# The first gate tile of each layer moved ahead of the transposes of the latents

## What is computed

```python
def token_mix(h, pos, w_in, lb, hg_norm_g, q_norm_g, w_q_up, kv_norm_g, w_kv_up, w_br_a, w_br_b, w_out):
    proj = h @ w_in
    hq, hf, hi, hgate, cq, ckv, kr, gates = jnp.split(proj, IN_SPLITS, axis=-1)
    o_a = hgrn2_mix(hq, hf, hi, lb)             # a recurrence, in levels
    ...
    y_b = mla_mix(cq, ckv, kr, pos, q_norm_g, w_q_up, kv_norm_g, w_kv_up) @ w_br_b
    g = jax.nn.sigmoid(gates.astype(jnp.float32))
    g_a, g_b = g[..., :D], g[..., D:]
    merged = (g_a * y_a + g_b * y_b)
    return merged @ w_out

def mla_mix(c_q, c_kv, k_rope, pos, q_norm_g, w_q_up, kv_norm_g, w_kv_up):
    q = (rmsnorm(c_q, q_norm_g) @ w_q_up)       # 384 latent columns
    kv = (rmsnorm(c_kv, kv_norm_g) @ w_kv_up)   # 256 latent columns
    ...
```

## Time and profile before

| | |
|---|---|
| median of 3 runs | 1886.56 us (1885.85 to 1888.33) |
| the profiled execution | 1887.39 us |
| its span | 1885.7 us |
| TensorE matmuls busy | 1693.9 us, 90% of the span |
| VectorE busy | 1184.9 us, 63% |
| ScalarE busy | 975.0 us, 52% |
| GpSimd busy | 26.7 us, 1% |
| moved by DMA | 401.83 MB, 213 GB/s over the span |

### The profile page before, as it was taken

One profiled execution on the slowest core, in us unless ns is written; L12 is line 12 of the kernel. 1 busy time (PEld: TensorE's weight loads), 2 busy tenths in 40 slices (PEclk: granted clock), 3 DMA queues, 4 the chain that ended last, 5 costly groups with the idle time before them and its releaser, 6 DMA issues.

```text
span 1885.7 us, 26698 instructions
## 1 busy us (share of the span) xinstructions
PE 1693.9 (90%) x10028; PEld 1408.3 (75%) x10028; DVE 1184.9 (63%) x1669; ACT 975.0 (52%) x1365; POOL 26.7 (1%) x58
## 2 busy tenths in 40 slices
PE   6999897899996989886899999979898769999995
PEld 6999785499995968743688888869695357888884
DVE  5544355554447444723788888854574378888886
ACT  4444344154434423401788888744341049888883
POOL 2000000000000000001000000000000010000000
PEclk9999998999998989998799999989899969999998
DMA  8555478845552559722398998935332308898992
GB/s 255 191 188 178 154 244 279 272 156 190 178 190 88 169 169 348 267 89 89 113 335 314 333 329 319 331 110 166 125 112 89 112 32 297 316 332 325 324 335 76
DMA packets 245831, 401.83 MB, mean 213 GB/s; under 512 B 6522, under 2 KB 151596, under 8 KB 245756
## 3 DMA queue, kind: packets, MB, share of 16 engines
q1 hardware_dynamic: 244792, 398.77, 61.6%
q0 software_dynamic: 592, 0.93, 0.2%
q10 hardware_dynamic: 372, 1.07, 0.2%
HBM read 399.70 MB, written 1.05 MB: 213 GB/s over the span
## 4 chain that ended last, share of the span: by engine, by line
PE 82%; DVE 10%; ACT 4%; issue 2%; DMA 1%; ACTq 0%; DVEq 0%
PE bank L1226 19%; PE bank L1168 14%; PE bank L1250 9%; PE bank L1097 8%; PE bank L1075 8%; PE bank L1181 6%; PE bank L1063 4%; PE bank L1262 3%; PE bank L1333 2%; DMA sb_ring<-in_w_in 1%; PE bank L1508 1%; PE bank L1086 1%; PE bank L1579 1%; DVE sb_w_lo L1808 1%; DVE sb_w_lo L1873 1%
## 5 line engine op out<-in xcount | busy, mean ns | idle before, releaser
L1873 DVE TENSOR_TENSOR sb_w_lo<-sb_ring,sb_moe_hi 128x1024 fp32r<-128x1024 f32 x384 | 448.4, 1220 | 29.5 <-ACT sb_moe_hi L697 29.2
L697 ACT ACTIVATE sb_moe_hi<-sb_ring 128x1024 fp32r<-128x1024 f32 x384 | 381.5, 1056 | 69.8 <-PE bank L1250 33.7
L1829 DVE TENSOR_TENSOR sb_w_lo<-sb_ring,sb_w_hi 128x1024 fp32r<-128x1024 f32 x128 | 151.1, 1222 | 172.1 <-ACT sb_w_hi L652 172.1
L1168 PE MATMUL bank<-sb_hT_hi,sb_w_hi 128*128 128x256 f32 x704 | 200.6, 285 | 3.6 <-DVE sb_hT_lo L1785 3.6
L652 ACT ACTIVATE sb_w_hi<-sb_ring 128x1024 fp32r<-128x1024 f32 x128 | 128.4, 1051 | 144.6 <-PE bank L1168 131.1
L1168 PE MATMUL bank<-sb_hT_hi,sb_w_lo 128*128 128x256 f32 x704 | 200.4, 285 | 0.0
L1168 PE MATMUL bank<-sb_hT_lo,sb_w_hi 128*128 128x256 f32 x704 | 200.4, 285 | 0.0
L1226 PE MATMUL bank<-sb_moe_hi,sb_xw_hi 128*128 128x512 f32 x480 | 193.6, 403 | 0.0
L1226 PE MATMUL bank<-sb_w_lo,sb_xw_hi 128*128 128x512 f32 x480 | 190.9, 398 | 0.0
L1226 PE MATMUL bank<-sb_moe_hi,sb_xw_lo 128*128 128x512 f32 x480 | 190.2, 396 | 0.0
L1250 PE MATMUL bank<-sb_moe_hi,sb_hid_hi 128*128 128x512 f32 x512 | 145.4, 396 | 2.9 <-DVE sb_hid_hi L1899 2.9
(11 more groups left out here) (465 smaller groups left out, 3132.9 us busy)
## 6 DMA issues: line engine op xcount, KB each, us to landing
sb_ring<-in_w_up SPq DMA_DIRECT2D x64, 1024.0 KB, 5.3
sb_ring<-in_w_gate SPq DMA_DIRECT2D x64, 1024.0 KB, 5.3
sb_ring<-in_w_down SPq DMA_DIRECT2D x64, 1024.0 KB, 4.8
sb_ring<-in_ada_w SPq DMA_DIRECT2D x48, 1024.0 KB, 7.7
sb_ring<-in_w_in SPq DMA_DIRECT2D x46, 1024.0 KB, 5.3
sb_ring<-in_ffn_w_in SPq DMA_DIRECT2D x44, 1024.0 KB, 5.0
sb_ring<-in_ffn_w_out SPq DMA_DIRECT2D x22, 1024.0 KB, 4.9
sb_ring<-in_w_out SPq DMA_DIRECT2D x12, 1024.0 KB, 5.0
```

Of the source, the lines that this page charges most:

```text
L697: A(moe_hi[:, q % 3, c], ring[:, at % RING, c], ACT.Copy).then_inc(s["moe_hi"], 1)
L1168: ins = mm(bank[4 + 2 * p + b][:, jj * SEQ:(jj + 1) * SEQ], w[wp][:, k, jj * P:(jj + 1) * P], h_parts[hp][:, k, :], start=k == 0 and m == ...
L1829: ins = tt(w_lo[:, slot, c], ring[:, slot, c], w_hi[:, q % 2, c].bitcast(F32), ALU.subtract)
L1873: ins = tt(w_lo[:, slot, c], ring[:, slot, c], moe_hi[:, q % 3, c].bitcast(F32), ALU.subtract)
```

## The change

The product with `gates0` is issued right behind `misc2`, before the wait for `latents`, into bank 3 instead of bank 0. Its eviction stands behind the square root and before the wait for the transposes. TensorE waits for that eviction before `kv_up` writes banks 0 to 3. In the list of tiles `gates0` comes right behind `misc2`. Step 0 keeps its `ada` products, its level and its part of the attention.

```diff
@@ -333,11 +333,14 @@
             for n in range(3):
                 tile(f"misc{n}.{l}", cols(w2, 2048 + MISC_AT[n], FB))
+            gates = lambda n: tile(f"gates{n}.{l}", cols(w2, 2048 + MISC + n * FB, FB))
+            gates(0)
             for n in range(2):
                 tile(f"q_up{n}.{l}", cols(a["w_q_up_2"][l], n * QL, QL))
             tile(f"kv_up.{l}", cols(a["w_kv_up_2"][l], 0, 1024))
             for n in range(8):
-                tile(f"gates{n}.{l}", cols(w2, 2048 + MISC + n * FB, FB))
+                if n:
+                    gates(n)
@@ -927,7 +930,13 @@
+                def gate_out(n, src):
+                    used(f"gates{n}.{l}")
+                    A(G[:, :, n // 4, (n % 4) * FB:(n % 4 + 1) * FB],
+                      src[:, :].rearrange("p (t c) -> p t c", t=T), ACT.Tanh, scale=0.5).then_inc(s["gates"], 1)
+
                 root(next(roots))
+                gate_out(0, bank[3])
                 act.wait_ge(s["cT"], run)
@@ -944,10 +953,8 @@
                 for n, L in enumerate(LEVELS):
 
-                    used(f"gates{n}.{l}")
-                    ins = A(G[:, :, n // 4, (n % 4) * FB:(n % 4 + 1) * FB],
-                            bank[n % 3][:, :].rearrange("p (t c) -> p t c", t=T), ACT.Tanh, scale=0.5)
-                    ins.then_inc(s["gates"], 1)
+                    if n:
+                        gate_out(n, bank[n % 3])
@@ -1490,6 +1497,7 @@
                 by_token(f"misc2.{l}", bank[2], hT_lo_l)
 
+                by_token(f"gates0.{l}", bank[3], hT_lo_l)
                 pe.wait_ge(s["latents"], run)
@@ -1508,6 +1516,7 @@
                     ins.then_inc(tiles_used, 1)
+                pe.wait_ge(s["gates"], 8 * l + 1)
                 pos = place[f"kv_up.{l}"]
@@ -1562,7 +1571,8 @@
-                    by_token(f"gates{n}.{l}", bank[n % 3], hT_lo_l)
+                    if n:
+                        by_token(f"gates{n}.{l}", bank[n % 3], hT_lo_l)
```

## The result

The change made the kernel faster, by less than was predicted: 1875.56 us median (12 runs, 1871.79 to 1883.5) against 1888.18 us for the kernel before (12 runs, 1885.49 to 1893.8), a ratio of 0.9937 with a 95% interval of 0.9925 to 0.995. That is 11.9 us (9.4 to 14.2); 18.6 had been predicted. The profiled execution took 1880.98 us, its span 1879.3. Timed again, beside the first experiments, the ratio was 0.9927 (0.9905 to 0.995), 13.8 us.

A forecast was written before the change was run, and what follows sets the result against it. The prediction took the chain of waits, 82% of it TensorE, to bound the kernel. Gains of 9.5 us in layer 0 and 9.1 in layer 1 make 18.6 us, so 1868.0 us, range 1865.0 to 1876.0.

The forecast's parts named there:

- The moved product: gates0's product, 5.94 (5.86) us, fits TensorE's 6.4 us gap before the latents transposes, with about 0.5 us left.
- The moved eviction: The Tanh on ScalarE, between the root and the latents' copies, costs 0, with a margin of 1.0 us.
- The clock: Full clock through the latents transposes and q_up: gains of 3.55 us in layer 0 and 4.05 in layer 1.
- The first rival: Chance 0.20: TensorE gets 1.2 GHz in the transposes or part of q_up, losing 1 to 7.6 us; 1869.5 to 1875.5.
- After kv_up: Behind kv_up gates0's 5.94 (5.86) us leave, the 2.41 us wait stays; layer 1 waits 0.7 us before gates1.
- Layer 0's loads: Layer 0's gate tile loads land 9.5 to 10.2 us earlier, so layer 0 keeps its 9.5 us gain.
- the prediction's own signs of being wrong: Transposes waiting beyond the latents' scaling, q_up showing 0.50, or layer 0's gates ending less than 8 us earlier.
- The sum: Over both layers, 9.5 + 9.1 = 18.6 us gained, giving 1868.0 us.
- The other rivals: Layer 0's loads eat its gain (0.10, 1877.5), larger gain (0.05, 1864), slower (0.02, 1898.2), nothing moves (0.01, 1886.6).
- a slower kernel: Chance 0.02: 1.2 GHz from the moved product through q_up costs 5.8 us a layer; 1898.2.
- The larger gain: Chance 0.05: with layer 0's loads 3 us further ahead, TensorE's 2.60 us pause and its dip go; 1864.

The follow-up runs named there:

- the filled version: Changed kernel plus 16 unread matmuls behind the ten latents transposes in each layer; 0.9907 of the kernel before, 0.9912 on the second occasion.
- the second further trace of the changed kernel: The changed kernel traced again without any edit, the second of three more traces; an execution of 1872.46 us.
- the half dose: Changed kernel plus 8 unread matmuls behind the latents transposes in each layer; 0.9915 of the kernel before, 16.1 us under it.
- a further version: Changed kernel with level 0's matmuls behind the transposes and gates1's product behind kv_up; 1868.97 us, 0.9883 of the kernel before; again 1866.7 us, 0.9872.
- the kernel with only the first gap filled: Kernel before, gates0 not moved, plus 48 unread matmuls between misc2 and the wait for the latents; 0.9989 of the kernel before, 2.1 us.

## Why the prediction was right or wrong

- **The moved product** was right: the gap was long enough, 0.6 us were left (0.5 predicted), and both parts of the weights were there.
- **The moved eviction** was right: cost 0, with a margin of 1.35 us (1.0 predicted).
- **The clock** is the step that failed, at the sentence "My case is the nearest in length to the first, so I take the full clock". The pause of 2.0 us behind the short transposes was enough for the clock to fall in all four traces of layer 1 and in three of four of layer 0. q_up took 10.2 and 9.6 us on average instead of 7.8. Of the 7.6 us given to the clock 3.8 were missing by the traces. At full clock q_up takes 8.0 us, not 7.8, and the transposes 1.3, not 1.2; that is another 0.6 us over both layers. The row that I set against it, the pause of 2.41 us without a fall, was one execution at one place: behind kv_up, the same 2.41 us do bring a fall in the filled version (the clock was 0.60 there in layer 1, from 1334.60 to 1338.90), and the second further trace of the changed kernel has one there too. So the step had one row for it and no reason why length alone should decide. The first rival, at 0.20, had the mechanism right and should have been the forecast. That the timed 11.9 us lie near its lower end (11.0 to 17.6) is in part chance: of the 6.7 us missing from the forecast, this term accounts for some 4, and the rest lay in stretches further on, which the rival didn't name.
- **After kv_up** was right: 2.41 us of wait stayed in both layers, and layer 1 has the new wait on VectorE's split, 0.41 us (0.7 predicted). It is 0.41 us whether q_up ran slowly (the first trace) or at full clock (the half dose), so the difference isn't the clock's.
- **Layer 0's loads** were right in kind: they moved with TensorE. In the first trace gates3 landed 6.7 us earlier where some 10 had been predicted, since TensorE itself had gained less. Where the clock held in layer 0 (the second further trace) it landed at 705.35, 9.8 us earlier against the first transposes, and the stage took 115.99 us against 116.1 predicted. Two of the prediction's own signs of being wrong came true in the first trace, and both by way of the clock: q_up showed 0.50, and layer 0's gate stage gained under 8 us.
- **The sum** by the first trace: 6.8 + 7.15 = 14.0 instead of 18.6 us in the gate stages. The timing gave 11.9 and 13.8. How the rest up to these numbers is made up is not resolved: the stretch between the layers is 4 us longer in one trace of the changed kernel than in another, the tail is some 3.5 us longer in a further version's first trace than in its second, and the kernel before spreads over 8 us in its own timed runs, of which its two traces, both of executions near 1887.5 us, show one point.
- **The other rivals**: none came. Nothing pointed to a slower kernel; the product ran at full clock behind the projections. The larger gain rested on the 2.60 us pause in layer 0 hanging on a landing. It doesn't: with gates3 landing 6.7 us and more earlier it is still 2.6 to 2.7 us long, and VectorE (L1993, now L2003) ends it.

## What to carry to other kernels

When work is moved into a pause to keep TensorE's clock up, look at every pause that is left until the next long product, not at the longest alone: here the clock fell in the next one, and what had been won at ten short transposes was lost again in a long product. A fill of unread matmuls costs a few lines, shows what the clock is worth before any real work is moved, and can itself be faster than idling. Whether the clock falls at a given pause differs from execution to execution, so one row is no rule, and a forecast that rests on it needs both cases.

## What the runs showed of the hardware that was not expected

A pause of 2.02 us between 1.3 us of transposes and dense work brought the granted clock down from 2.4 to 1.2 GHz in seven of eight places of the changed kernel, and in both of the kernel with only the first gap filled; one of 1.07 us in none of two. And the spread of this kernel's times, 11 us or 0.6%, is for the greater part the clock (9.9 of 10.8 us are longer busy time of the same matmuls): even ahead of the change, up to layer 0's latents, the same work took from 660.85 to 664.98 us in four traces of one kernel.
